# Expert rows of a gathered mixture: one 8 KB transfer a row split into two of 4 KB, in two rings

## The reference, cut to what matters

```python
def chunk(xc):                                   # 128 tokens
    q = (xc @ w_q).reshape(tc, PEER_HEADS, 2, PEER_DQ // 2)
    s = jnp.einsum('thpd,hpkd->thpk', q, sub_keys)
    s_top, i_top = lax.top_k(s, PEER_TOPK)
    ...
    best, pos = lax.top_k(cand..., PEER_TOPK)    # 16 of 256 candidates
    expert = jnp.take_along_axis(cand_idx..., pos, axis=-1)
    gate = jax.nn.softmax(best, axis=-1)
    ue = jnp.take(expert_u, expert, axis=0)      # up rows
    ve = jnp.take(expert_v, expert, axis=0)      # down rows
    h = jax.nn.gelu(jnp.einsum('thkd,td->thk', ue, xc), approximate=False)
    return jnp.einsum('thk,thkd->td', (gate * h), ve)
```

## Time and profile before

| | us |
|---|---|
| median of 3 runs | 1660.76 |
| lowest and highest run | 1657.38, 1661.72 |
| the profiled execution, its own time | 1656.79 |
| its span in the trace | 1655.0 |
| first transfer of a row issued | 447.91 |
| last transfer of a row issued | 1099.17 |
| first copy after the last row's matmuls | 1141.13 |

### The profile page before, as it was taken

The page is one execution under the profiler, slowest core; times in us unless marked ns, Lnnn a source line. Parts: engine busy times, 40 slices in busy tenths (PEclk is TensorE's granted clock), DMA queues, the critical chain, the costliest instruction groups (busy, mean ns, idle before and its releaser), DMA issues. The chain is left out here.

```text
span 1655.0 us, 18102 instructions
## 1 busy us (share of the span) xinstructions
PE 1355.6 (82%) x6762; PEld 928.1 (56%) x6762; DVE 1017.8 (62%) x2352; ACT 404.4 (24%) x842; POOL 289.1 (17%) x297
## 2 busy tenths in 40 slices
PE   4796789997888787877877878765799968799988
PEld 2783477767853332332322223223688857699988
DVE  0597377774867868786868696542422487455542
ACT  1513300014521010101010101003523434554431
POOL 0002100000124343434443434420000000000000
PEclk9897798899899999999999999996899989899989
DMA  9346831137179999999999999992244205434543
GB/s 400 151 152 251 327 124 61 51 130 291 53 276 419 415 422 412 422 417 421 401 423 407 422 410 421 421 423 125 89 166 160 95 1 204 153 129 177 203 153 128
DMA packets 48184, 426.59 MB, mean 258 GB/s; under 512 B 5344, under 2 KB 5472, under 8 KB 5600
## 3 DMA queue, kind: packets, MB, share of 16 engines
q0 software_dynamic: 36864, 268.45, 39.4%
q1 hardware_dynamic: 11232, 156.98, 24.4%
HBM read 424.36 MB, written 1.05 MB: 257 GB/s over the span
## 5 line engine op out<-in xcount | busy, mean ns | idle before, releaser
L1232 PE MATMUL bank<-arena 128*128 128x512 f32 x1024 | 512.7, 638 | 151.6 <-DVE arena L1328 151.5
L1232 PEld LDWEIGHTS bank<-arena 128*128 128x128 f32 x1024 | 189.2, 199 | 470.2 <-DVE arena L1328 299.7
L1352 DVE CUSTOM_DVE_ANT_0 arena<-arena 128x1024 f32<-128x1024 f32 x256 | 313.1, 1223 | 176.0 <-DMA arena<-experts_in,arena 175.5
L1185 POOL DMA_INDIRECT arena<-experts_in,arena x256 | 268.3, 1048 | 629.1 <-PE bank L1232 373.5
L459 PE MATMUL bank<-rounded,rounded 128*128 128x256 f32 x1136 | 331.4, 292 | 56.3 <-DVE rounded L422 47.2
L460 PE MATMUL bank<-rounded,rounded 128*128 128x256 f32 x1136 | 328.0, 289 | 0.0
L461 PE MATMUL bank<-rounded,ring_r 128*128 128x256 f32 x1136 | 327.9, 289 | 0.0
L436 DVE TENSOR_TENSOR ring_r<-ring,rounded 128x1024 fp32r<-128x1024 f32 (+2 forms) x136 | 170.9, 1270 | 177.2 <-ACT rounded L431 177.2
L459 PEld LDWEIGHTS bank<-rounded,rounded 128*128 128x128 f32 x1136 | 223.6, 197 | 59.7 <-issue 38.2
L460 PEld LDWEIGHTS bank<-rounded,rounded 128*128 128x128 f32 x1136 | 224.4, 197 | 0.5 <-issue 0.5
L461 PEld LDWEIGHTS bank<-rounded,ring_r 128*128 128x128 f32 x1136 | 223.0, 196 | 0.0
(11 more groups left out here) (239 smaller groups left out, 1086.1 us busy)
## 6 DMA issues: line engine op xcount, KB each, us to landing
ring<-slots_in SPq DMA_DIRECT2D x73, 2048.0 KB, 8.4
arena<-experts_in,arena POOLq DMA_INDIRECT x256, 13.6
xT<-xT_in SPq DMA_DIRECT2D x1, 1024.0 KB, 15.8
mixT<-slots_in SPq DMA_DIRECT2D x1, 1024.0 KB, 6.8
out_dram<-xT SPq DMA_DIRECT2D x1, 1024.0 KB, 3.9
con<-consts_in SPq DMA_DIRECT2D x1, 552.0 KB, 13.7
vec<-vecs_in SPq DMA_DIRECT2D x1, 167.0 KB, 2.4
```

Of the source, the lines that this page charges most:

```text
L1185: pool.indirect_dma_start(rows[:, r % GRING, :], None, experts_in, bass.IndirectOffsetOnAxis(ap=expert[:, tt, at:at + 1], axis=0)).then_in ...
L1232: ins = pe.matmul(psum[2 * tt + half][:, :], diag[:, r % DIAGS, :], rows[:, r % GRING, D + 512 * half:D + 512 * half + 512], start=(h == 0 ...
L1352: dve.tensor_tensor_reduce(rows[:, r % GRING, 0:D], rows[:, r % GRING, 0:D], utok[:, tt, :], 1.0, 0.0, ALU.mult, ALU.add, hdot[:, r:r + 1] ...
```

## The change

The host hands over two tables, `experts_u` and `experts_v`, 4 KB a row each. POOL issues two indirect transfers for a row, each 4 KB a partition (0.5 MB), with the same indices: first the up rows into the ring `rows_u`, then the down rows into the ring `rows_v`. Each ring has 8 slots of half the size, so both together take the place of `rows`. The slot of `rows_u` is free when DVE has dotted the row (`dotted`), the slot of `rows_v` when PE has used it (`rows_used`). DVE waits for the first transfer only; PE gets a wait of its own for the second, ahead of its wait for the diagonal matrix.

```diff
-        rows = area(ROWS_AT, GRING, 2 * D)
+        rows_u = area(ROWS_AT, GRING, D)
+        rows_v = area(ROWS_AT + GRING * D, GRING, D)
...
+        row_v_loaded = [sem(f"row_v_loaded{j}") for j in range(GRING)]
...
                             r = row_of(h, tt, k)
+                            at = h * TOPK + k
+                            if r >= GRING:
+                                pool.wait_ge(dotted, r - GRING + 1)
+                            pool.indirect_dma_start(rows_u[:, r % GRING, :], None, experts_u,
+                                                    bass.IndirectOffsetOnAxis(ap=expert[:, tt, at:at + 1], axis=0)
+                                                    ).then_inc(row_loaded[r % GRING], 16)
                             if r >= GRING:
                                 pool.wait_ge(rows_used, r - GRING + 1)
-                            at = h * TOPK + k
-                            pool.indirect_dma_start(rows[:, r % GRING, :], None, experts_in,
+                            pool.indirect_dma_start(rows_v[:, r % GRING, :], None, experts_v,
                                                     bass.IndirectOffsetOnAxis(ap=expert[:, tt, at:at + 1], axis=0)
-                                                    ).then_inc(row_loaded[r % GRING], 16)
+                                                    ).then_inc(row_v_loaded[r % GRING], 16)
...
+                            pe.wait_ge(row_v_loaded[r % GRING], 16 * (r // GRING + 1))
                             pe.wait_ge(diag_ready, r + 1)
                             for half in range(2):
                                 ins = pe.matmul(psum[2 * tt + half][:, :], diag[:, r % DIAGS, :],
-                                                rows[:, r % GRING, D + 512 * half:D + 512 * half + 512],
+                                                rows_v[:, r % GRING, 512 * half:512 * half + 512],
...
                             dve.wait_ge(row_loaded[r % GRING], 16 * (r // GRING + 1))
-                            dve.tensor_tensor_reduce(rows[:, r % GRING, 0:D], rows[:, r % GRING, 0:D], utok[:, tt, :],
+                            dve.tensor_tensor_reduce(rows_u[:, r % GRING, :], rows_u[:, r % GRING, :], utok[:, tt, :],
```

More of the change, by code:

```diff
@@ L118, in shape_constants, with build @@
     return c, rope
-def build(nc, xT_in, vecs_in, consts_in, slots_in, experts_in, out):
+def build(nc, xT_in, vecs_in, consts_in, slots_in, experts_u, experts_v, out):
     with ExitStack() as ctx:
@@ L1933 @@
     fill("w_down", w["w_down_2"][0], P)
-    experts = np.concatenate([w["peer_u"][0], w["peer_v"][0]], axis=1)
     xT = np.ascontiguousarray(w["x"][0].T.reshape(KT, P, T).transpose(1, 0, 2))
     nc = bacc.Bacc("TRN2", target_bir_lowering=False, num_devices=1)
-    arrays = {"xT_in": xT, "vecs_in": vecs, "consts_in": consts, "slots_in": slots, "experts_in": experts}
+    arrays = {"xT_in": xT, "vecs_in": vecs, "consts_in": consts, "slots_in": slots, "experts_u": np.ascontiguousarray(w["peer_u"][0]),
+              "experts_v": np.ascontiguousarray(w["peer_v"][0])}
     args = [nc.dram_tensor(k, a.shape, mybir.dt.from_np(a.dtype), kind="ExternalInput").ap()
```

## The result

The kernel after the change takes 1742.24 us (median of 4 runs, 1739.85 to 1749.09) against 1659.07 for the one before on the same chip (4 runs, 1657.11 to 1661.72): ratio 1.0507, 95% interval 1.047 to 1.0543. It is slower, as forecast, 18 us above the forecast 1724 and inside 1682 to 1788.

A forecast was written before the change was run, and what follows sets the result against it. Before, the DMA engines bound at 2.485 us a row; after, POOL's issues at 2.80. 1656.8 + 76.9 (slower rows) - 10 (stage's end) = 1723.7, forecast 1724 us, 8-in-10 range 1682 to 1788.

The forecast's parts named there:

- Bytes and number of issues: Expert stage gathers: bytes stay, 256 issues become 512 at 0.94 us plus 0.30 between, a floor of 2.48 us a row.
- What lifts POOL off the floor: POOL issues begun in a dot's first 1.09 us end 0.81 us after it, making the mean row 2.80 us.
- POOL is not stopped: Ring slots: eight rows last 22.4 us, a down slot needs 14.6; DVE's longest pause, 5.9 us, is under the 7.8 difference.
- Pace: POOL's mean time a row in the expert stage after the change: 2.80 us, against the DMA engines' 2.485.
- End: Stage's end: POOL's last 3 to 4 rows pass beside the slot loads, last issue to ACT's copy 32 us; -10 us.
- about as much is outstanding: Stage's end: when the slot loads start, pending data is about as before, so the end comes as long after, 34.3 us.
- the first term: Expert stage from row 10 on: 246 rows at 2.80 us, from 487.3 to 1176.1 instead of 1099.17, +76.9 us.
- Signs forecast: Profile signs expected in the expert stage: mean issue about 1.10 us, POOL issues busy some 560 us, plateau about 375 GB/s.
- Rival A: POOL's issues and dots never meet or cost little: mean row 2.60 us, 1675 us in all; chance 0.12.
- B: Dots meet POOL's issues badly: mean row 3.0 us, 1773 us, at the limit 1870; chance 0.08 together with D.
- C: Faster: the up slot freed early lets POOL have half a row more under way, 1640 to 1652 us; chance 0.06.
- D: DMA engines move 4 KB packets slower; up to 10% (2.73 us a row) hidden by POOL's 2.80; chance 0.08 with B.

The follow-up runs named there:

- Experiment 5: Kernel before plus a second indirect transfer per row, 64 bytes a partition over 128 partitions, to scratch nobody reads: 1747.24 us, ratio 1.0538.
- experiment 7: Kernel after, but each half transfer brings 1 KB a partition instead of 4 KB, the rest zero: 1733.83 us, ratio 1.0448.
- 1: Kernel after, but both halves wait for PE's use of the row, so the up ring's separate release is gone: 1749.48 us, ratio 1.0569 to kernel before.
- Experiment 10: Kernel before plus one tiny extra indirect transfer on every second row, 384 issues: 1665.49 us, ratio 1.0055.
- experiment 2: Kernel after with a plain one-input sum over the up row in place of DVE's dot: 1738.13 us, ratio 1.0483 to kernel before.
- 8: Kernel after with a plain sum for the dot and the diagonal matrix made on ACT: 1744.56 us, ratio 1.0527 to kernel before.
- 11: Kernel before plus a second tiny indirect transfer per row covering 32 partitions, not 128: 1685.69 us, ratio 1.0165.
- 12: Kernel before plus one POOL memset of 128 x 1024 behind each row from the ninth on: 1670.57 us, ratio 1.0082.
- 6: Kernel after with the diagonal matrix made by two ACT activations a row instead of DVE: 1747.62 us, ratio 1.059 to kernel before.
- 9: Kernel before plus two tiny indirect transfers per row, 768 issues: 2033.23 us (2 runs), ratio 1.2269.
- experiment 4: Kernel before, with the four 2 MB slot loads waiting until three rows are left instead of eight: 1634.68 us, ratio 0.9852.

## Why the prediction was right, and where it was not

*Bytes and number of issues: right.* Same bytes, 144 packets and a floor of 0.94 + 0.30 us for a half as for a whole row. Experiment 5 shows that the second issue alone is enough, 7 that bytes aren't part of it, 1 that the separate release isn't. Experiment 10, with 2.1 us of issuing a row against 2.485 us of data, lost only 9 us.

*What lifts POOL off the floor: the mechanism is there, its size was 0.32 us a row (2.80 - 2.48) and measured 66 / 256 = 0.26, and it is not the price.* Issues do end 0.80 to 0.83 us after a dot, 217 of them. But without them (2, 8) the kernel is hardly faster or not at all. The forecast took each lost microsecond for one that could be had back; in these kernels pauses fill the place of the stretches.

*"POOL is not stopped": this step failed.* It counted a down slot as free 14.6 us after its issue, when PE's matmuls end, against 22.4 us for eight rows, and took the 7.8 us between them for enough. The way from the matmul's end to the waiting engine was put at nothing. In the kernel after it took up to 12.8 us, and POOL stopped for `rows_used`, either at once (653.70) or because DVE had stood for a late count of its own and PE lacked matrices (582.35, 966.63 and 768.83, the last shown below): 54.8 - 9.7 = some 45 us of longer gaps behind the start, 0.17 us a row.

*Pace.* Predicted 2.80 us from row 10 on, measured (1200.48 - 488.62) / 246 = 2.89, begin 488.62 for 487.3. That is 0.09 x 246 = 22 us too little: the stretches smaller by 0.06, the pauses larger by 0.17 a row.

*End.* Predicted -10 us, measured -17.9. Two assumptions failed against each other. POOL's last issue comes 2.7 us behind the loads (1200.48 - 1197.76), not some 10. And "about as much is outstanding" is wrong: from the loads to the last dot it is 18.3 us (1216.09 - 1197.76), not 34.3, since a POOL that is the bound leaves only a row or two on their way. To the copy that makes 24.1 us from the last issue, not 32. The terms together: +76.9 became +101.3, -10 became -17.9; 1656.8 + 83.1 = 1739.9, the profiled execution's 1739.85. That the forecast came within 18 us is partly luck: the first term was 24.4 us too small, and the second took 7.9 of that back.

*Signs forecast.* Mean issue about 1.10 (1.07), POOL's issues busy some 560 us (547.8), gaps mostly "issue" (494 of 511 by number), issues that end 0.81 after a dot (yes), plateau about 375 GB/s (two stretches with 356, slices 305 to 398), clock 1.00 in quiet stretches (yes). Rival A is out, its favourable phase did not come. B's time wasn't reached. C was decided against by the half's issue, no cheaper than a whole one's (1.07 against 1.048). D is out: at a quarter of the data the loss stays.

So the forecast named the right resource and came near the sum, but it put all that lies above the floor on the lock, and the experiments don't bear that out.

**What stays open.** Why the counts come late. The runs show that it happens with two indirect transfers a row over 128 partitions, not with the second over 32 (11) or with a memset in its place (12), that it doesn't depend on bytes (7), on what DVE does (2, 6, 8) or on the rings (1, 5), and that it catches DVE's counts as well as PE's. It isn't there at three issues a row (9), at an even shorter mean of 1.37 us an issue; so issues close to each other don't bring it about by themselves, and I have no account of it. The seven traces that show it also lack many updates, so that whether the recording of the trace has a part in it is open too. The Trainium skill, "Perfetto Trace Analysis", section "DMA Instruction — SWDGE (GPSIMD)", says that the recorded end of such an issue is when its last descriptor is written, ahead of the end of the program that writes them. That leaves room for unseen work, but no run here shows it. Not tried were a ring of more slots, which would show what the late counts cost, the same number of transfers at an enforced larger distance, and other lists of experts.

## What to carry to other kernels

Price a gather by its indirect transfers, not only by its bytes: in these kernels POOL's issues over 128 partitions follow each other by 1.37 to 1.48 us in the mean when there are two or three a row, though a single one shows 0.94 us. A second issue a row cost 5%, one on every other row 0.55%. To find out beforehand, add a tiny transfer that nobody reads: it showed the whole loss without the rewrite. When a cost that you see in the trace is taken away and the time stays, sum all losses of that engine before and after; here stretches and pauses changed places. When pauses look unexplained, see which wait of the kernel they stand in front of, and whether they move when the wait is moved: here they did. And look at what a prefetch takes from the last transfers on the critical path: starting it five rows later made the kernel before 23 us faster.

## What the runs showed of the hardware

In the seven kernels with 512 issues over 128 partitions, increments of a semaphore reach the engines that wait up to 17.1 us after the instruction that makes them (experiment 7; 12.8 in the kernel after), while in the seven others the updates of `rows_used` are recorded 12 to 15 ns after it. Another form of it, in the timeline of the kernel after:

```profile
757.11 0.94 POOL L1192 DMA_INDIRECT arena<-experts_v,arena  x1 [0.30 <-issue]
...
760.85 0.94 POOL L1187 DMA_INDIRECT arena<-experts_u,arena  x1 [0.30 <-issue]
762.22 0.20 DVE L1301 CAST uT<-uT 128x64 f32<-128x64 uint32 x1 [6.20 <-remote]
...
768.83 0.94 POOL L1192 DMA_INDIRECT arena<-experts_v,arena  x1 [7.04 <-PE bank L1240]
```

Here DVE alone stands for 6.20 us before a small conversion, while POOL issues each 1.245 us, and the conversion starts 0.43 us after POOL's last issue has ended. It waits for DVE's own count of its operations (`tk_ready`): the last of them ended at 756.03, and the trace records increments at 756.45, 759.27 and 762.09. The gap of 7.04 us at 768.83 is this stall passed on: PE had no matrices for 15.5 us and freed no slot. In the same trace an issue begun in a dot's first 1.08 us ends 0.80 to 0.83 us after the dot. The Trainium skill, "SBUF — State Buffer", section "Who interferes with whom", tells of an exclusive lock between DVE and GpSimd, and the traces agree: 217 issues ended by the dot's end, none stretched by a sum over one input (experiment 2). The long stalls are waits for late counts, PE's among them; whether the lock has a part in the lateness, no run here decides.

Slot loads of 2 MB take the larger part of the DMA engines from the gathers: rows of 1.05 MB that come 2.49 us apart alone come 7.4 apart beside four such loads, 142 GB/s of the 349 that the core moves from 1111 to 1133 us; in experiment 4, where the loads start later, the last rows stay 2.49 apart.
